# Two channel blocks of convolution products stand ahead of the attention steps, in two banks

## What is computed

```python
proj = h @ w_in[layer]
q, kc, vc, ksl, vsl, kwn, vwn, gts, cb, cc, ch = jnp.split(proj, split_at, axis=-1)
...
o_attn = nsa_attention(q, kc, vc, ksl, vsl, kwn, vwn, gts, rel_bias)   # compressed, selected, window branch
z = cc * ch;  y = conv3(z);  o_conv = cb * y                          # short_conv, per channel
mixed = concat([rms_norm(o_attn), rms_norm(o_conv)])
x = x + mixed @ w_out[layer]
```

## Time and profile before

| what | value |
| --- | --- |
| median of 3 runs | 2018.73 us (2018.65 to 2019.4) |
| the profiled execution | 2017.98 us, of which the span is 2016.2 us |
| PE busy | 1994.3 us (99%) |
| weight loads (PEld) busy | 1458.9 us (72%) |
| DVE busy | 656.9 us (33%) |
| ACT busy | 313.3 us (16%) |
| granted PE clock, mean | 1.000 |
| conv products (L1713), both layers | 181.3 us busy, 384 MATMULs |
| chain that ended last | PE 95%, DVE 2%, the rest 1% or less each |

### The profile page before, as it was taken

How to read it: one execution, slowest core, us unless ns; L and a number is a source line. 1 busy time by engine, 2 the same in 40 slices (tenths; PEclk the granted TensorE clock), 3 DMA queues, 4 the chain that set the end, 5 groups by cost and what they waited for, 6 DMA issues and landing times.

```text
span 2016.2 us, 29955 instructions
## 1 busy us (share of the span) xinstructions
PE 1994.3 (99%) x12645; PEld 1458.9 (72%) x12645; DVE 656.9 (33%) x1375; ACT 313.3 (16%) x808; POOL 97.3 (5%) x103
## 2 busy tenths in 40 slices
PE   8999999999999999999999999999999999999999
PEld 4455548888864444555499974899999999975655
DVE  5366644333234353656420000000000000055463
ACT  3243311111100023433100001100000000011110
POOL 2100010000000011000020000000000000000120
PEclk9999999999999999999999999999999999999999
DMA  7510112222240134100099559977787777878993
GB/s 277 188 42 2 43 49 94 84 84 84 104 168 0 65 139 164 43 1 1 32 344 358 220 222 374 389 277 259 283 297 275 290 280 283 294 273 301 346 344 123
DMA packets 48231, 377.82 MB, mean 187 GB/s; under 512 B 6501, under 2 KB 6677, under 8 KB 20834
## 3 DMA queue, kind: packets, MB, share of 16 engines
q1 hardware_dynamic: 40960, 356.04, 46.3%
q0 software_dynamic: 5872, 15.89, 2.8%
q10 hardware_dynamic: 1266, 3.97, 0.5%
HBM read 367.28 MB, written 10.77 MB: 188 GB/s over the span
## 4 chain that ended last, share of the span: by engine, by line
PE 95%; DVE 2%; issue 1%; DMA 1%; ACT 1%; POOL 0%; ACTq 0%; DVEq 0%; SPq 0%; POOLq 0%
PE ps L657 23%; PE ps L1905 13%; PE ps L675 11%; PE ps L1713 7%; PE ps L1921 7%; PE ps L826 6%; PE ps L1837 5%; PE ps L1621 5%; PE ps L811 3%; PE ps L720 2%; PE ps L1793 2%; PE ps L1781 2%; PE ps L1641 1%; PE ps L738 1%; PE ps L1768 1%
## 5 line engine op out<-in xcount | busy, mean ns | idle before, releaser
L657 PE MATMUL ps<-work,arena 128*128 128x136 f32 (+4 forms) x3712 | 477.3, 287 | 0.0
L657 PEld LDWEIGHTS ps<-work,arena 128*128 128x128 f32 x3712 | 464.9, 190 | 2.7 <-issue 2.5
L675 PE MATMUL ps<-hid,arena 128*128 128x136 f32 (+2 forms) x1760 | 236.1, 287 | 0.0
L1038 DVE TENSOR_TENSOR hid<-sg,ps 128x136 f32<-128x136 f32 (+4 forms) x116 | 35.3, 305 | 607.9 <-ACT sg L1300 607.6
L675 PEld LDWEIGHTS ps<-hid,arena 128*128 128x128 f32 x1760 | 225.1, 190 | 0.8 <-issue 0.8
L1713 PE MATMUL ps<-hT,arena 128*128 128x512 f32 x384 | 181.3, 596 | 2.6 <-DVE arena L2227 2.5
L1905 PE MATMUL ps<-hT,arena 128*128 128x256 f32 x704 | 155.7, 379 | 0.0
L1905 PEld LDWEIGHTS ps<-hT,arena 128*128 128x128 f32 x704 | 133.7, 190 | 18.6 <-issue 0.5
L1300 ACT ACTIVATE sg<-ps 128x136 f32<-128x136 f32 (+4 forms) x116 | 33.8, 292 | 612.9 <-PE ps L657 609.7
L1905 PE MATMUL ps<-work,arena 128*128 128x256 f32 x528 | 117.6, 379 | 0.8 <-issue 0.8
L1837 PE MATMUL ps<-arena 128*128 128x512 f32 x256 | 114.3, 594 | 1.1 <-DVE x L2386 1.0
(11 more groups left out here) (368 smaller groups left out, 1883.5 us busy)
## 6 DMA issues: line engine op xcount, KB each, us to landing
arena<-m_w SPq DMA_DIRECT2D x132, 1536.0 KB, 7.1
arena<-m_w SPq DMA_DIRECT2D x44, 1024.0 KB, 8.6
arena<-f_gu SPq DMA_DIRECT2D x11, 2048.0 KB, 8.0
arena<-m_w SPq DMA_DIRECT2D x44, 512.0 KB, 5.8
arena<-w_cv SPq DMA_DIRECT2D x8, 1536.0 KB, 15.1
arena<-w_o SPq DMA_DIRECT2D x4, 2048.0 KB, 7.2
arena<-f_dn SPq DMA_DIRECT2D x4, 2048.0 KB, 8.4
arena<-w_q SPq DMA_DIRECT2D x4, 1024.0 KB, 7.6
```

The costliest lines, as they stand in the source:

```text
L657: m = mm(ps[:, bank_of(i, s), j * CAP:j * CAP + W], w[:, k, :], xT[:, k, 0:W], start=(k == 0), stop=(k == KD - 1))
L675: m = mm(ps[:, 2 + j // 2, (j % 2) * CAP:(j % 2) * CAP + W], down_w[s % NSLOT][:, j * P:(j + 1) * P], hid[:, s % 2, 0:W], start=(s == 0 an ...
```

## The change

Ahead of the steps now stand 48 products, six thirds, that is blocks 0 and 1 whole, by fills of 8, 4, 5, 3 and 28; the steps hold the other 48, two in each of steps 0 to 17 (one per fill) and three in each of steps 18 to 21. The first five thirds alternate between bank 1 and bank 3, so that a third waits for the reader of the last but one; from the sixth on all use bank 3. Behind the fill of 28 PE waits until z of block 1 has been read from bank 1, which scores need. DVE does both blocks' work ahead of its first score reduction, except the second block's sum of squares, which goes to step 1; ACT does both blocks' copies and outputs ahead of its first exponential. The places of conv work for blocks 2 and 3 follow from `THIRD_END`: thirds 6 to 11 end in steps 3, 7, 11, 15, 19 and 21 (before, thirds 6 to 11 ended in steps 9, 11, 13, 15, 18 and 21).

```diff
--- before.py
+++ after.py
@@ -71,13 +71,14 @@
 O_SQUARES = {p + 1: t for p, t in CMP_VALUES.items()}
 O_REDUCE = {p + 2: t for p, t in CMP_VALUES.items() if t < TT - 1}
 O_TOTAL = {p + 4: t for p, t in CMP_VALUES.items() if t < TT - 1}
-STEP_FILL = 16 * ((2, 2, 0),) + 2 * ((1, 1, 0), (2, 1, 0), (2, 1, 0))
-assert sum(sum(f) for f in STEP_FILL) == 10 * KD and len(STEP_FILL) <= NP
+BEFORE = 6
+STEP_FILL = 18 * ((1, 1, 0),) + 4 * ((2, 1, 0),)
+assert sum(sum(f) for f in STEP_FILL) == (3 * CT - BEFORE) * KD and len(STEP_FILL) <= NP
 
 
 def third_ends():
 
-    ends, n = {}, 2 * KD
+    ends, n = {}, BEFORE * KD
     for p, f in enumerate(STEP_FILL):
         for _ in range(sum(f)):
             n += 1
@@ -87,9 +88,10 @@
 
 
 THIRD_END = third_ends()
+THIRD_BANK = (1, 3, 1, 3, 1) + (3 * CT - 5) * (3,)
 EARLY_OUT = {NP - 2: ((0,), ()), NP - 1: ((1,), (2, 3))}
 assert len(STEP_FILL) == NP - 2
-assert sorted(THIRD_END.values()) == list(range(2, 3 * CT))
+assert sorted(THIRD_END.values()) == list(range(BEFORE, 3 * CT))
 
 
 SLOT = 3 * KD * P
@@ -1700,23 +1702,24 @@
                         third, k = divmod(given[0], KD)
                         i, j = third // 3, (1, 2, 0)[third % 3]
                         if k == 0:
-                            if third == 0:
+                            back = third - (2 if third < BEFORE else 1)
+                            if third <= 1:
                                 pe.wait_ge(proj_summed, quarter_of(L, SUM_KV1, 1))
-                            elif j == 2:
-                                pe.wait_ge(cc_done, CT * L + i + 1)
-                            elif j == 0:
-                                pe.wait_ge(zc_done, CT * L + i + 1)
+                            elif back % 3 == 0:
+                                pe.wait_ge(cc_done, CT * L + back // 3 + 1)
+                            elif back % 3 == 1:
+                                pe.wait_ge(zc_done, CT * L + back // 3 + 1)
                             else:
-                                pe.wait_ge(cv_done, CT * L + i)
+                                pe.wait_ge(cv_done, CT * L + back // 3 + 1)
                             if j == 1:
                                 pe.wait_ge(wcv_in[CO[i]], 16 * (L + 1))
-                        m = mm(ps[:, 3, :], cv_w[CO[i]][:, k, j * P:(j + 1) * P], hT[:, k, :], start=(k == 0), stop=(k == KD - 1))
+                        m = mm(ps[:, THIRD_BANK[third], :], cv_w[CO[i]][:, k, j * P:(j + 1) * P], hT[:, k, :], start=(k == 0), stop=(k == KD - 1))
                         if k == KD - 1:
                             m.then_inc(pcv_done, 1)
                         given[0] += 1
 
                 q_turn(3)
-                fill(4)
+                fill(8)
                 pe.wait_ge(gate_copied, L + 1)
                 for t in range(TT):
                     m = mm(ps[:, 2, 24 * t:24 * (t + 1)], gate_part[:, t * P:(t + 1) * P], cst[:, C_SUM:C_SUM + 24], start=True, stop=True)
@@ -1747,6 +1750,8 @@
                         m = mm(ps[0:NCMP, 7, (2 * a + g) * DH:(2 * a + g + 1) * DH], hidc[:, a * DH + 32 * g:a * DH + 32 * g + NCMP],
                                pc[:, PC_W2 + a * DH:PC_W2 + (a + 1) * DH], start=True, stop=True)
                 m.then_inc(ho_done, 1)
+                fill(28)
+                pe.wait_ge(zc_done, CT * L + 2)
 
                 def cmp_keys():
                     pe.wait_ge(kcn_done, L + 1)
@@ -2209,7 +2214,7 @@
                 def conv_z(i):
                     dve.wait_ge(pcv_done, 3 * CT * L + 3 * i + 2)
                     dve.wait_ge(cc_done, CT * L + i + 1)
-                    v.tensor_tensor(zc[:, 2:S + 2], ccb[:, :], ps[:, 3, :], ALU.mult).then_inc(zc_done, 1)
+                    v.tensor_tensor(zc[:, 2:S + 2], ccb[:, :], ps[:, THIRD_BANK[3 * i + 1], :], ALU.mult).then_inc(zc_done, 1)
 
                 def conv_taps(i, first=True, last=True):
                     w = lambda j: pc[:, PC_CONV + 3 * CO[i] + j:PC_CONV + 3 * CO[i] + j + 1]
@@ -2224,7 +2229,7 @@
 
                 def conv_b(i):
                     dve.wait_ge(pcv_done, 3 * CT * L + 3 * i + 3)
-                    v.tensor_tensor(yc[:, :], yc[:, :], ps[:, 3, :], ALU.mult).then_inc(cv_done, 1)
+                    v.tensor_tensor(yc[:, :], yc[:, :], ps[:, THIRD_BANK[3 * i + 2], :], ALU.mult).then_inc(cv_done, 1)
 
                 def conv_sum(i):
                     dve.wait_ge(cvm_done, CT * L + i + 1)
@@ -2241,6 +2246,11 @@
                 v.memset(Pc[:, :, :], 0.0).then_inc(pc_zeroed, 1)
                 conv_z(0)
                 conv_taps(0)
+                conv_b(0)
+                conv_sum(0)
+                conv_z(1)
+                conv_taps(1)
+                conv_b(1)
 
                 def cmp_keys():
                     reduce_heads(L, 8, NCMP)
@@ -2345,6 +2355,7 @@
                         cmp_keys()
                     if p == 1:
                         cmp_vals()
+                        conv_sum(1)
                     if p in O_SQUARES:
                         evacuate(O_SQUARES[p])
                     if p in O_REDUCE:
@@ -2615,7 +2626,7 @@
                     se.wait_ge(pcv_done, 3 * CT * L + 3 * i + 1)
                     if CT * L + i:
                         se.wait_ge(sqs_done, CT * L + i)
-                    nc.scalar.copy(ccb[:, :], ps[:, 3, :]).then_inc(cc_done, 1)
+                    nc.scalar.copy(ccb[:, :], ps[:, THIRD_BANK[3 * i], :]).then_inc(cc_done, 1)
 
                 def conv_out(i):
                     c = CO[i]
@@ -2631,6 +2642,9 @@
                 nc.scalar.copy(hidc[:, :], ps[:, 5, 256:256 + P]).then_inc(hid_copied, 1)
                 se.wait_ge(ho_done, L + 1)
                 square(L, 8, ps[0:NCMP, 7, 0:2 * DH], NCMP, 2 * DH)
+                conv_out(0)
+                conv_c(1)
+                conv_out(1)
 
                 def cmp_keys():
                     se.wait_ge(kct_ps, L + 1)
```

## The result

The changed kernel takes **2050.28 us** (median of four runs, 2049.96 to 2051.01), the kernel before 2018.69 us beside it: a ratio of 1.0156, interval 1.0143 to 1.0169. It is slower by 31.6 us; the profiled execution's span grew by 32.1 us, from 2016.2 to 2048.3 us.

The account below looks back on a forecast made before the run. PE was taken to set the pace of steps 0 to 15. Terms 3.1 + 2.7 + 0.7 + 3.8 + 3.85 + 0.4 + 0 - 1.25 = 13.3 us a layer, 26.6 in both, gave 2045.3 us, range 2030 to 2054.

Parts of the forecast that it names:

- Entry: Steps 0 to 3: block 1's work and the table load delay the second turn and step 3's values, 3.1 us a layer.
- Loop in steps 4 to 7: With two products fewer per step, PE's values wait for the chain through DVE and ACT's copy, 2.7 us a layer.
- Steps 8 to 15: Loop waits 0.7 us and DVE's long steps 3.8 us, less 1.25 for step 14's B multiplication wait that goes.
- Seam: Step 19: product 89 waits for DVE's z of block 3, last in its queue; 4.0 less 0.15, 3.85 us.
- Step 22: First output products meet block 3's B multiplication, which ends 0.75 us later: 0.4 us a layer.
- The 28 products ahead: Fill ahead of the steps: no wait in these products and none at third 9.
- Rival 2: Moved products cost less ahead than in the steps, hiding DVE and ACT waits; not slower, 2018 us; chance 5%.
- Rival 1: Only ordered waits count: entry, seam and step 22 remain, less 1.25; 6.1 us a layer, 2031 us; chance 13%.
- the long steps: Steps 8, 9, 12 and 13, where DVE's extra work makes turns wait; 3.8 us a layer, at least 0.
- The clock, a term of 0: No cost from a lower PE clock; PE was granted 1.00 even in the first 10 us, busy 2.18.
- the rival: Clock falls behind step 19's wait, rest of steps 19 and 20 twice as long; 17.6 us more, 2063; chance 8%.

Follow-up runs that it names:

- the copy's experiment: Changed kernel with ACT's copy of half of the turned weights moved between the step's two exponential passes: 2042.63 us.
- DVE's long steps split: Changed kernel with block 2's taps whole in step 10, its sum and tile 1's square sums in step 14: 2045.54 us.
- all four edits: Changed kernel with block 10 ending in step 18, copy between exponentials, block 1's output passes and sum later, DVE's steps 9 and 13 dealt out: 2020.74 us.

## Why the prediction was right, and where it was not

The forecast was slower, 2045.3 us in a range of 2030 to 2054, and the time is 2050.3. Point by point:

- **Entry, 3.1 us a layer:** right. The brackets are 0.22, 0.36, 2.08 and 0.45 us, 3.11 together, and the stretch lost 3.33. The table load stands behind the output passes, as it was put.
- **Loop in steps 4 to 7, 2.7 us:** right in place and sum (2.52). The brackets show less, 0.64, 0.64 and 0.50 in steps 5 to 7: a bracket leaves out the overlap of neighbouring groups that a wait also breaks (0.07 us at step 5's values, see the copy's experiment). The round into step 8, put at 0.45, shows no bracket: the compressed scores (0.96 us from 165.93) stand ahead of the values there, as they do in step 4.
- **Steps 8 to 15, 0.7 + 3.8 - 1.25:** right as a sum, 3.51 against 3.25. Step 9's turn waits 1.49 (forecast 1.55), steps 10 and 13 0.57 and 0.61, step 14 0.39 at the values and 0.41 at the turn; step 14's old wait is gone. The loop's own share does not show by itself.
- **Seam, 3.85 us:** right, 4.06 where the clock stayed up. **Step 22, 0.4 us:** wrong, it costs nothing. A bracket of 0.21 us stands at its output products, but the 0.28 us that the scores of step 23 waited before is gone, and the step takes 4.74 us in both kernels.
- **The 28 products ahead:** no wait among them and none at third 9, as it was put; 24.23 us for 28 products. Rival 2 falls: these products cost 0.865 us each, as in the steps, and the four more that the first fill holds inside the dense stretch lengthen it by 3.43 us (80.44 to 83.88 before, 81.03 to 87.90 after). By the Trainium skill (Perfetto Trace Analysis, Identifying the Most-Contended Engine) matmul busy time is a poor measure of headroom; here the full busy time of that stretch was a true bound, since those four products found no room in it.
- **Rival 1** (only the waits of the written order, 2031) falls: taking out the loop's waits and those of the long steps gave 7.7 and 4.7 us.
- **The clock, a term of 0: this step failed.** The forecast left it at no cost because PE was granted 1.00 in the first 10 us at 2.18 us of work, and priced the rival at 17.6 us. Both were off. The first row was no evidence either way, as two rows of the kernel before show that lie in it and right behind it:

```profile
7.82 3.28 PE L1593 MATMUL ps<-cst,work 128*128 128x128 f32 x16 [7.82 <-DVE work L2079]
...
15.64 1.09 PE L1593 MATMUL ps<-cst,work 128*128 128x128 f32 x8
```

Sixteen transposes take 3.28 us where eight of the same take 1.09 later. From 8.30 to 10.22 they start 0.21 us apart, as the turns do at 232.62 in the changed kernel, where the grant is 0.50 (four in 1.06 us). So PE went at half pace there although the row grants 1.00; why the column reads so, the trace doesn't show.

The clock did fall behind the wait in step 19 of both layers and behind step 2's in layer 1. Against the same stretches where it stayed up that costs 2.93 us (steps 16 to 21 in layer 0, 40.53 less 37.60), 1.65 us (the same steps of layer 1, 920.46 to 959.71, 39.25 less 37.60) and 1.13 us (steps 0 to 3 of layer 1, 839.89 to 856.37, 16.48 us against 15.35 in layer 0): **5.7 us**, against a miss of 5.0. The rival had the mechanism right and the stay wrong: it took the whole rest of steps 19 and 20 at the lower level in both layers, and the rows show 6 us of it in layer 0 and 3.4 in layer 1 (4 us at a mean of 0.57).

The Trainium skill (TensorE: Matmul & The Clock Gate, HAM oscillation) says that each group behind a long enough wait starts at the lower clock. The runs agree in part: behind the wait of 3.77 us the clock fell in nine of ten cases, but in five of these only about 1 us after the next products had begun (with the copy moved they begin at 230.14 and the grant is 1.00 up to 231.3), and it fell behind some waits of 2.08 us as well.

The sum closes on the rows of both layers. In layer 0 the stretches lost 3.33 + 2.52 + 3.51 + 6.99 = 16.35 us. In layer 1 the scores of steps 0, 4, 8, 16 and 22 start at 795.30, 814.55, 840.43, 893.38 and 926.92 before and at 839.89, 856.37, 877.81, 920.46 and 959.71 after, which makes 15.88 us in the same way. Of the 32.2 us together 26.5 are waits, against 26.6 forecast, and 5.7 the clock. Ahead of the steps of layer 0 stand 0.6 us more (81.03 in place of 80.44 at the first product), and behind them a wait of 1.4 us for a load became one of 0.7 us for DVE; that leaves 32.1, and the spans differ by 32.1. That the waits fit to 0.1 us is in part luck: step 22's 0.4 us a layer did not come, the long steps cost 0.26 us more than their terms, and layer 1 does not repeat layer 0 row by row, since a wait of 0.38 us for a B multiplication in its step 2 went too.

## What to carry to other kernels

Filler work between dependent steps is cover: ahead of removing it, follow the chain beside the busy engine round once, from the instruction that starts it, and compare it with what is left of the engine's own way. Let the last piece of a block end with a step, since a next block that begins in the same step waits for whatever the reader's engine has queued ahead of the read. And give a new wait of some microseconds on PE a second term for the clock behind it, between nothing and what a short stay at half pace costs.

## What the runs showed of the hardware

The clock's fall behind a wait of PE is short, and not the same in each execution. In the profiles taken here it fell behind 9 of 10 waits of 3.77 or 3.78 us in step 19 (all but layer 0 with DVE's long steps split), behind none of the two of 2.85 us and none of the two of 0.78 us in the same place, but behind 6 of 10 waits of 2.08 us in step 2, ahead of which PE had other, shorter waits. Two of these ten stand in one execution of the changed kernel with the same work ahead: PE was busy for 7.53 us from 130 to 140 in layer 0, where the grant stayed at 1.00, and for 7.54 us from 841.5 to 851.5 in layer 1, where it fell at 851.2. So neither the length of the last wait nor the amount of work ahead of it decides it alone; what else does was not isolated.

How long PE stays at the lower level makes the price. In the changed kernel it was granted 0.50 from 230.00 to 236.75, a stay that began inside the wait, and from 943.40 to 946.80, one that began with the products behind it: 2.93 and 1.65 us. One fall costs 1.1 to 2.9 us where it was measured. The spread of the runs of one kernel goes with the mean clock: 2041.84 us at 0.998 and 2049.37 us at 0.995, while the kernel with all four edits, whose longest step wait is 0.9 us, keeps within 1.9 us.
